# Sparse attention: sums of the softmax from ones beside the values, and the output scaled behind the product instead of the probabilities

## The reference, cut to what matters

```python
q = q.reshape(T, 4, 64)          # four heads; one key and one value for all (64 wide)
s = einsum('qhd,kd->hqk', q, k) / 8
s = where(chosen, s, -1e30)      # chosen: the 256 best keys of each query, causal by chunks of 64
p = softmax(s, axis=-1)          # exp(s - max) / sum
o = einsum('hqk,kd->qhd', p, v)
```

## Time and profile before

| | |
|---|---|
| median of 3 runs | 3217.14 us (3216.52 to 3218.18) |
| the profiled execution | 3217.15 us, of which the span is 3215.4 us |
| TensorE busy | 3026.0 us, 94% of the span |
| VectorE, ScalarE, GpSimd busy | 42%, 30%, 32% |
| sparse attention, from the end of its first query product to the first matmul of the merge | 2068.2 to 2194.9 us of the span |

### The profile page before, as it was taken

One profiled execution on the slowest core, in us unless ns is written; L12 is line 12 of the kernel. 1 busy time (PEld: TensorE's weight loads), 2 busy tenths in 40 slices (PEclk: granted clock), 3 DMA queues, 4 the chain that ended last, 5 costly groups with the idle time before them and its releaser, 6 DMA issues.

```text
span 3215.4 us, 38366 instructions
## 1 busy us (share of the span) xinstructions
PE 3026.0 (94%) x14387; PEld 2425.6 (75%) x14387; DVE 1356.6 (42%) x2160; ACT 952.7 (30%) x1569; POOL 1013.3 (32%) x797
## 2 busy tenths in 40 slices
PE   5999989999999999999989999978978999999998
PEld 2888768888876877888767888746766888888886
DVE  3344430111011035544397999851275233332425
ACT  3354532222222244232254222243333111111113
POOL 1544312323421345122212333302445332332323
PEclk9999999999999999999999999989988999999999
DMA  5211021111122122110111111102121111111111
GB/s 193 54 37 37 11 82 52 47 51 43 44 66 75 48 87 92 51 27 26 36 44 29 49 47 49 39 1 84 58 66 40 47 46 51 46 52 46 46 52 72
DMA packets 261410, 170.53 MB, mean 53 GB/s; under 512 B 23556, under 2 KB 249404, under 8 KB 260157
## 3 DMA queue, kind: packets, MB, share of 16 engines
q1 hardware_dynamic: 259442, 163.76, 17.1%
q10 hardware_dynamic: 1867, 5.41, 0.4%
HBM read 160.69 MB, written 8.45 MB: 53 GB/s over the span
## 4 chain that ended last, share of the span: by engine, by line
PE 82%; issue 8%; DVE 6%; ACT 2%; POOL 1%; DMA 1%; ACTq 0%; POOLq 0%; DVEq 0%
PE ps L321 64%; PE ps L3498 2%; PE ps L3497 2%; PE ps L3499 2%; PE ps L2363 2%; DVE score L2944 1%; PE ps L939 1%; PE ps L530 1%; PE ps L953 1%; POOL w_lo L305 1%; DVE ssq L1868 1%; DVE h_lo L1858 1%; PE ps L1449 1%; PE ps L1452 1%; DMA rows<-in_norm_ffn_post 0%
## 5 line engine op out<-in xcount | busy, mean ns | idle before, releaser
L321 PE MATMUL ps<-h_hi,w_hi 128*128 128x512 f32 x2880 | 1148.8, 399 | 54.0 <-POOL w_lo L305 23.3
L321 PE MATMUL ps<-h_lo,w_hi 128*128 128x512 f32 x2880 | 1131.1, 393 | 0.0
L321 PE MATMUL ps<-h_hi,w_lo 128*128 128x512 f32 x2880 | 1129.6, 392 | 0.0
L305 POOL TENSOR_TENSOR w_lo<-raw,w_hi 128x512 fp32r<-128x512 f32 (+2 forms) x556 | 659.7, 1208 | 1388.6 <-ACT w_hi L298 1388.4
L321 PEld LDWEIGHTS ps<-h_hi,w_hi 128*128 128x128 f32 x2880 | 546.7, 190 | 178.0 <-issue 41.6
L321 PEld LDWEIGHTS ps<-h_hi,w_lo 128*128 128x128 f32 x2880 | 546.2, 190 | 117.0
L321 PEld LDWEIGHTS ps<-h_lo,w_hi 128*128 128x128 f32 x2880 | 547.0, 190 | 113.7 <-issue 3.1
L298 ACT ACTIVATE w_hi<-raw 128x512 fp32r<-128x512 f32 (+2 forms) x556 | 288.3, 567 | 899.3 <-PE ps L321 676.1
L3447 DVE TENSOR_TENSOR act<-gate,ps 128x1024 f32<-128x1024 f32 x22 | 26.9, 1221 | 444.9 <-PE ps L321 444.9
L3456 DVE TENSOR_TENSOR acc<-acc,ps 128x1024 f32<-128x1024 f32 x160 | 195.4, 1221 | 29.8 <-PE ps L3499 29.8
L1153 DVE TENSOR_TENSOR part<-sig,ps 128x1024 f32<-128x1024 f32 x40 | 48.6, 1215 | 355.4 <-PE ps L321 275.0
(11 more groups left out here) (416 smaller groups left out, 3544.2 us busy)
## 6 DMA issues: line engine op xcount, KB each, us to landing
raw<-in_w_in SPq DMA_DIRECT2D x88, 512.0 KB, 4.0
raw<-in_w_ffn_gate_up SPq DMA_DIRECT2D x44, 512.0 KB, 3.8
raw<-in_w_out SPq DMA_DIRECT2D x32, 512.0 KB, 3.7
raw<-in_w_gate SPq DMA_DIRECT2D x32, 512.0 KB, 3.6
raw<-in_w_ffn_down SPq DMA_DIRECT2D x22, 512.0 KB, 3.5
w_ada<-in_w_ada SPq DMA_DIRECT2D x8, 1024.0 KB, 5.1
x_tok<-in_x ACTq DMA_DIRECT2D x1, 4096.0 KB, 20.6
residual_gate<-in_w_ada SPq DMA_DIRECT2D x8, 512.0 KB
```

Source lines behind the costliest of these rows:

```text
L305: pool.tensor_tensor(w_lo[:, s, cut], raw[:, s, cut], w_hi[:, s, cut].bitcast(F32), ALU.subtract).then_inc(split.sem, 1)
L321: last = pe.matmul(dst, w[:, chunk[0] % 2, k], x(k), start=(k == ks[0] and n == 0), stop=(k == ks[-1] and n == 2))
```

## The change

It takes the division out of the probabilities.

- The right half of each value tile is no longer the values again but ones, written by POOL behind its wait for ScalarE's copy. So the rows 64 to 127 of the product `ps[3]` hold the sum of the exponentials of each query and head, 64 times over; the rows 0 to 63 hold the output before the division.
- `exps` has no `accum_out`, and TensorE waits with the first turn of a step for the exponentials, not for normalised probabilities.
- `normalise(n)` now works behind the last `weigh` of step n, and stands in DVE's list one step later: a reciprocal of 64x512 sums into `inverse`, and two multiplications of 64x256 into `y32`. Both lie in the part of `score` that belongs to step 1, which is read by then. It signals `h_ready`.
- ScalarE's copy to `y_hi_t` and DVE's `rest_o` read `y32`, one instruction of 128x256 each, and ScalarE waits for `h_ready`.
- The queries are taken out of `ps` in halves of 512 tokens, as each half of `product` ends. TensorE's wait for `q_parts` stands directly ahead of the scores, and it waits for the ones ahead of the loop.

```diff
-                stat = sb(sc, "stat", [P, 2, 4, H])
+                stat = sb(sc, "stat", [P, 2, 2, H])
...
+                    return ps[3][0:64, c:c + 2 * P].rearrange("p (t c) -> p t c", c=P)
+                def sums_of(n):
+                    return ps[3][64:P, n % 2 * HALF:n % 2 * HALF + HALF]
+                spare = score[:, score_at(order[1]):score_at(order[1]) + keys_of(order[1])]
+                inverse = spare[0:64, 0:H * P]
...
                     pool.memset(edge[0:64, keys_of(1) - 64:], NEG).then_inc(aux.sem, 1)
+                    pool.wait_ge(tr_evicted.sem, tr_evicted.at(2))
+                    pool.memset(v_two[:, :, 1], 1.0).then_inc(aux.sem, 1)
                     for m in range(2):
                         rest_chunk(pool, m + 1, 0, 2)
...
-                    for n in range(2):
-                        last = act.activation(v_two[:, :, n], v, ACT.Copy)
-                    last.then_inc(tr_evicted.sem, 1)
+                    act.activation(v_two[:, :, 0], v, ACT.Copy).then_inc(tr_evicted.sem, 1)
...
-                        act.activation(x, x, ACT.Exp, bias=stat[:, n % 2, 1, h:h + 1],
-                                       accum_out=stat[:, n % 2, 2, h:h + 1]).then_inc(exped.sem, 1)
+                        act.activation(x, x, ACT.Exp, bias=stat[:, n % 2, 1, h:h + 1]).then_inc(exped.sem, 1)
...
-                        act.wait_ge(o_ready.sem, o_ready.at(turns.index((n, b)) + 1))
-                        for half in range(2):
-                            rows = slice(half * 64, half * 64 + 64)
-                            last = act.activation(y_hi_t[rows, :, b * P:b * P + P], out_of(n, half), ACT.Copy)
-                        last.then_inc(y_hi.sem, 1)
+                        act.wait_ge(h_ready.sem, h_ready.at(n + 1))
+                        act.activation(y_hi_t[:, :, b * P:b * P + P], y32(n), ACT.Copy).then_inc(y_hi.sem, 1)
...
                     def normalise(n):
-                        dve.wait_ge(exped.sem, exped.at(n * H + H))
-                        dve_steps.done(dve.reciprocal(stat[:, n % 2, 3], stat[:, n % 2, 2]))
+                        dve.wait_ge(o_ready.sem, o_ready.at(turns.index((n, order[n])) + 1))
+                        dve_steps.done(dve.reciprocal(inverse, sums_of(n)))
                         dve_steps.wait(dve)
-                        for first, to in pieces(n):
-                            x = prob_of(n)[:, :, first * P:to * P]
-                            dve.tensor_tensor(x, x, stat[:, n % 2, 3].rearrange("p (h k) -> p h k", k=1).broadcast_to(list(x.shape)),
-                                              ALU.mult).then_inc(probs.sem, 1)
+                        for half in range(2):
+                            last = dve.tensor_tensor(y32(n)[half * 64:half * 64 + 64], out_of(n, half),
+                                                     inverse[:, half * 2 * P:half * 2 * P + 2 * P].rearrange("p (t c) -> p t c", c=P), ALU.mult)
+                        last.then_inc(h_ready.sem, 1)
...
                         if n + 1 < TT:
                             bias_scores(n + 1, (0, 1))
-                        normalise(n)
+                        if n >= 1:
+                            normalise(n - 1)
                         if n + 1 < TT:
                             bias_scores(n + 1, (2, 3))
                         if n >= 1:
                             rest_o(n - 1)
+                    normalise(TT - 1)
                     rest_o(TT - 1)
...
-                            pe.wait_ge(o_evicted.sem, o_evicted.at(n - 1))
+                            pe.wait_ge(h_ready.sem, h_ready.at(n - 1))
...
+                    pe.wait_ge(aux3.sem, aux3.at(4))
                     score_heads(0, 0)
                     score_heads(0, 2)
+                    pe.wait_ge(aux.sem, aux.at(3))
                     for n in range(TT):
                         if n + 1 < TT:
                             score_heads(n + 1, 0)
-                        normed = sum(len(pieces(o)) for o in range(n))
+                        pe.wait_ge(exped.sem, exped.at(n * H + H))
                         for j in range(order[n] + 1):
-                            if j in [first for first, _ in pieces(n)]:
-                                normed += 1
-                                pe.wait_ge(probs.sem, probs.at(normed))
                             turn(n, j)
```

More of the change, by code:

```diff
@@ L3068, in out_of, with y32, q_ready @@
                     c = n % 2 * HALF + half * 2 * P
[L3069 to L3074, removed]
+                    return ps[3][0:64, c:c + 2 * P].rearrange("p (t c) -> p t c", c=P)
[3 more added lines that the diff above has]
+                inverse = spare[0:64, 0:H * P]
+                def y32(n):
+                    return spare[:, H * P + n % 2 * 2 * P:H * P + n % 2 * 2 * P + 2 * P].rearrange("p (t c) -> p t c", c=P)
+                def q_ready(engine, m, c):
+                    if c == 0:
+                        engine.wait_ge(sum_ready.sem, sum_ready.at(m + 1))
+                    else:
+                        engine.wait_ge(used.sem, after(used, m, 0, 2))
                 def prob_of(n):
@@ L3107, in _ @@
                             round_chunk(act, 2, 0, 2)
[L3108 to L3112, removed]
+                        for c in range(2):
+                            q_ready(act, m, c)
+                            for odd in range(2):
+                                rows = slice(odd * 64, odd * 64 + 64)
+                                last = act.activation(q_parts[rows, 2 * m + odd, c * HALF:c * HALF + HALF], ps[m][rows, c * HALF:c * HALF + HALF],
+                                                      ACT.Copy)
+                            last.then_inc(evicted.sem, 1)
                     def exps(n, h):
@@ L3153, in _ @@
                     for m in range(2):
[L3155 to L3159, removed]
+                        for c in range(2):
+                            dve.wait_ge(evicted.sem, evicted.at(2 * m + c + 1))
+                            cols = slice(c * HALF, c * HALF + HALF)
+                            for odd in range(2):
+                                rows, other, h = slice(odd * 64, odd * 64 + 64), slice(64 - odd * 64, P - odd * 64), 2 * m + odd
+                                last = dve.tensor_tensor(q_parts[other, h, cols], ps[m][rows, cols], q_parts[rows, h, cols].bitcast(F32),
+                                                         ALU.subtract)
+                            last.then_inc(aux3.sem, 1)
                     dve_steps.wait(dve)
@@ L3192, in rest_o @@
                         b = order[n]
[L3193 to L3197, removed]
+                        dve.tensor_tensor(y_lo_t[:, :, b * P:b * P + P], y32(n), y_hi_t[:, :, b * P:b * P + P].bitcast(F32), ALU.subtract)\
+                            .then_inc(o_evicted.sem, 1)
                     bias_scores(0, range(H))
@@ L3213, in _ @@
                     pe.wait_ge(*gates[0])
-                    product(pe, (0, 0, 2), wide(ps[0])).then_inc(used.sem, 1)
+                    product(pe, (0, 0, 2), wide(ps[0]), part=(0, 2)).then_inc(sum_ready.sem, 1)
+                    product(pe, (0, 0, 2), wide(ps[0]), part=(1, 2)).then_inc(used.sem, 1)
                     pe.wait_ge(*gates[1])
@@ L3224, in _ @@
                     split_ready(pe, 1, 0, 2)
-                    product(pe, (1, 0, 2), wide(ps[1])).then_inc(used.sem, 1)
-                    pe.wait_ge(aux3.sem, aux3.at(2))
+                    product(pe, (1, 0, 2), wide(ps[1]), part=(0, 2)).then_inc(sum_ready.sem, 1)
+                    product(pe, (1, 0, 2), wide(ps[1]), part=(1, 2)).then_inc(used.sem, 1)
                     pe.wait_ge(aux2.sem, aux2.at(1))
@@ L3281, in sparse_attention @@
             X = len(turns)
-            for s, n in ((aux, 2), (aux2, 1), (aux3, 2), (transposed, 1), (tr_evicted, 2), (evicted, 2), (scores, TT * H), (biased, TT * H), (mod_ready, TT * H),
-                         (exped, TT * H), (probs, sum(len(pieces(n)) for n in range(TT))), (pt_ready, X), (pt_evicted, X), (o_ready, X), (o_evicted, TT), (y_hi, TT)):
+            for s, n in ((aux, 3), (aux2, 1), (aux3, 4), (transposed, 1), (tr_evicted, 2), (evicted, 4), (sum_ready, 2), (h_ready, TT), (scores, TT * H), (biased, TT * H), (mod_ready, TT * H),
+                         (exped, TT * H), (pt_ready, X), (pt_evicted, X), (o_ready, X), (o_evicted, TT), (y_hi, TT)):
                 s.passed(n)
```

## The result

The changed kernel takes 3242.86 us (median of 4 runs, 3240.96 to 3245.62), the kernel before 3217.66 us in the same comparison: a ratio of 1.0076, 95% interval 1.0065 to 1.0088. It is 25 us slower, where 3 us faster was forecast and a range of 3207 to 3223 us was given. The span of the profiled execution is 3241.5 us.

The account below looks back on a forecast made before the run. Bound by TensorE (94% share) waiting in the loop for DVE's normalised probabilities, 22.7 us, then running at half clock. Terms +3.7 +2.3 -1.9 -4.4 -3.0 +2.2 +0.8 = -0.3, replay -2.6: 3214.5 us, range 3207 to 3223 us.

Parts of the forecast that it names:

- part 4: Steps 2 to 7: the wait moves to ScalarE's output copy, chain 2.65 us; -3.0 us, against it +2.2 us half clock.
- the reciprocal is slow per column: Rival: the 64x512 reciprocal, eight times on the chain, takes 4.4 us, giving 3244 us; chance 0.20.
- Part 1: Stage start: POOL's memset of the ones delays chunk 1's w_lo, +3.7 us, and half clock behind that wait, +2.3 us.
- Part 2: Before the scores: queries taken in halves leave 2.7 us behind the last query product instead of 4.63, -1.9 us.
- Part 3: Steps 0 and 1: first score matmul of step 1 to its first product takes 11.5 us instead of 15.9, -4.4 us.
- Part 5: Stage end: the output is whole later, about 3.05 us instead of 2.29 behind the merge's first matmul, +0.8 us.
- The sum: All terms against the profiled 3217.15 us: -0.3 us by full charges, -2.6 us with the replay, predicted 3214.5 us.
- the full charges: The sum with every half-clock cost counted in full: -0.3 us over the whole kernel.
- the replay's 2.3: Another 2.3 us less from replaying the lists: the slow stretch after step 1's wait is gone, that wait breaking in two.
- The half clock in the loop: In five steps, transposes no longer use up part of the slow stretch; +2.2 us charged, between 0 and 4.4.
- The rival of the clock: Loop waits break in two, two to four half-clock stretches fewer: -5 to -9 us more, about 3208 us; chance 0.15.
- The rival that the loop gives nothing: Beyond steps 0 and 1, ScalarE held for the output makes exponentials late: the -3.0 us is lost, 3220 us; chance 0.20.

Follow-up runs that it names:

- e1: The change with a multiplication of the same 64x512 by one in place of the reciprocal (computes something else): 3215.75 us, ratio 0.9991 to the kernel before.
- e2: The change with the reciprocal made twice in each step, one behind the other: 3269.16 us, ratio 1.0154 to the kernel before.
- e8: The change with nine more unused reciprocals, 1 to 256 columns wide, at the end of VectorE's list behind the output's signal: 3246.70 us (one run).
- e5: The kernel before with only the queries taken out of ps in halves: 3217.62 us, ratio 0.9998.
- e4: The change with ScalarE's copy of a step's output moved behind the next step's fourth (or last) turn: 3200.45 us, ratio 0.9945 to the kernel before.
- e7: The change with output copy behind the next step's fourth (or last) turn, ones memset behind chunk 1's rest, multiplication by one for the reciprocal: 3190.59 us.

## Why the prediction was wrong

**The step that failed is one term of part 4: the reciprocal of 64x512, "I take 0.71 us", with an upper bound of 1.2 us.** It measured 3.36 us, and it stands eight times on the chain (e1, e2). The mechanism of the loss was in the prediction as the rival "the reciprocal is slow per column", with a chance of 0.20, the place, the count of eight, the threshold of 1.8 us and 3244 us as its time; measured are 3242.86. That time is partly a coincidence: the rival had 4.4 us for the instruction, the real one is 3.36, and TensorE's longer busy time at the lower clock (5.7 us in e1's comparison) makes up most of the difference.

Why the price was misread can be seen in e8. I compared two groups of small reciprocals, 163 ns for one column and 170 ns for four, and took 7 ns for three columns. The two come from different places of the program, and the first is a mean over 64 instructions that differ among themselves (149 ns the shortest, 164 the median). In one place, back to back, it is 150 and 171 ns: 7 ns a column, three times what I read. The form of one column alone ranges from 149 to 167 ns in that trace, as wide as the 20 ns in question, so a row of 512 columns could not be had from it; the honest upper bound for an unseen width was several microseconds, and with it the range should have reached to the rival's time. On the two pages of the Trainium skill: an iterative divide "with a repeat count of 8" ("VectorE: DVE Perf Modes", section "First, the fixed hardware budget") pointed the right way; the trace disagrees with eight cycles as a price if a plain column takes 1.05 ns ((690 - 154)/511 by the earlier trace rows), as it shows 6.3 ns, six plain columns. One element in each cycle, as I read "Vector Engine (DVE) Microarchitecture Reference", section "3.2 Anatomy of a single slice", is refuted.

Point by point, by the prediction's own steps:

- *Part 1, the start on POOL, +3.7 and +2.3 us*: right in kind. From the stage's start to chunk 1 it takes 6.4 us (2077.75 - 2071.33) against 2.7 (2070.96 - 2068.24): +3.7 us. The half clock behind it covered some seven matmuls and not eleven: about 1.5 us.
- *Part 2, -1.9 us*: 2.91 us in place of 4.63, -1.7 us; alone in e5 2.71 us.
- *Part 3, -4.4 us (11.5 us from the first score of step 1 to its first product)*: 13.9 us in the change, whose reciprocal lies in it; with the assumed price, in e1, 11.47 us (2092.67 to 2104.14).
- *Part 4, the wait changes its owner*: right, and the chain of 2.65 us plus the reciprocal's excess meets the trace within 0.05 us in step 2. "The transposes' waits nearly vanish": 22.7 to 2.3 us.
- *Part 5, +0.8 us*: right but for the reciprocal. From the merge's first matmul to `res` it takes 5.79 us (2222.88 - 2217.09) instead of 2.29, +3.5 us, of which 2.65 are the reciprocal's excess; in e1 it is 3.11 us, +0.8. The wait for the chunk behind `res` grows by the same, from 4.36 to 7.89 us.
- *The sum*: by its own price it was good. e1 is 3.3 us faster than the kernel before, where 2.6 was forecast, and its stage is 4.3 us shorter: +3.6 us up to the first scores (forecast +4.1), -4.9 from there to the first product of step 1 (-4.4), -3.9 in the rest of the loop (-0.8 by the full charges, -3.1 with the replay's 2.3), +0.8 at the end (+0.8).
- *The half clock in the loop, +2.2 us in part 4*: no such loss is seen. With the forecast's price TensorE is busy for 94.85 us up to the merge (e1), 98.15 before: 3.3 us less for as many matmuls, somewhat more than the 2.5 us by which like stages differ.
- *The rival of the clock* could not show in the change, where the waits grew: 0.81 in the loop's stretch instead of 0.84. In e1, with an instruction as short as the forecast had the reciprocal, the clock did recover, from 0.85 to 0.89 up to the merge, but that came to 3.3 us and not to the further 5 to 9 us of the rival. *The rival that the loop gives nothing, with ScalarE making the exponentials late*: in e1 the gain is there, and the transposes wait only 2.3 us in all for exponentials in the change; it is out.

What the prediction did not ask is why ScalarE has to make the copy at that place. It took the order as given and so missed most of what the change can give: with the copy moved (e4) the slow reciprocal lies beside the turns, and the kernel is 19 us faster than before, not 3. With the memset moved too and a short instruction in the reciprocal's place it would be 28 us (e7).

## What to carry to other kernels

An operation moved from small tiles to a wide one needs a price per column measured on a wide tile; two small forms from different places don't give it, and a range must then reach to the worst price. When a product of an engine is moved off the waited-for path, look at who picks it up: a copy that nobody needs soon, standing in an in-order list ahead of one that everybody needs, puts the whole delay back on the path. Moving that copy behind the urgent work shortened the stage by 40 us here, more than a short instruction in place of the slow one (27 us).

## What was not expected of the hardware

- The reciprocal on VectorE costs 6.3 ns a column from 1 to 512 columns (150 ns, 545 ns at 64, 1746 ns at 256, 3359 ns at 512), where a multiplication of the same 64x512 from `ps` takes 693 ns.
- Shortening eight instructions by 21.3 us in all shortened the stage by 26.9 us. TensorE's busy time for the same matmuls fell with it from 100.56 to 94.85 us and its granted clock rose from 0.84 to 0.89; in e4 the clock is 0.94 over the stage, and TensorE is busy for 88.74 us up to the merge.
- The unchanged part of the program ahead of the stage took between 2067.6 and 2072.0 us over ten executions of ten kernels. The stage itself took 151.55 and 154.18 us with the same lists (the change and e8), by TensorE's busy time and clock alone. So effects of one or two microseconds are not shown by one profile of each kernel, only by the rows in which they lie.
